# A two-layer hybrid backbone step: the next head pair's r, k, v projections moved into a pair's tail, four-quadrant small matmuls, and low weight halves made by accumulating transfers

## The reference, cut to what matters

```python
h = rmsnorm(x, g_pre) * (1 + sc1) + sh1          # sc, sh, g: rows of silu(c) @ ada_w + b
z = h @ w_in                                     # projections of three mixers, and gates
out_a = rwkv7(dwconv3(z[r, k, v, w, a, g]))      # bidirectional delta-rule scan, 8 heads of 64
out_b = neighbourhood_attention(z[q, k, v])      # or dense, for the context; softmax
out_c = chunkwise_retention(z[q, k, v, g])       # bidirectional
merged = sum(sigmoid(z[gate_i]) * out_i @ w_o_i)
x = x + g1 * rmsnorm(merged @ w_out, g_post)
h2 = rmsnorm(x, g_ffn) * (1 + sc2) + sh2
x = x + g2 * rmsnorm((gelu(gate) * val) @ ffn_down, g_post2)  # gate, val = split(dwconv3(h2 @ ffn_up))
```

## Time and profile before

| | |
|---|---|
| median of 3 runs | 2025.21 us (2020.05 to 2028.73) |
| the profiled execution | 2030.75 us, span 2028.6 us |
| PE busy | 1905.9 us (94%) |
| DVE, ACT, POOL busy | 1001.8, 939.8, 944.0 us |
| moved by DMA | 231.52 MB, mean 114 GB/s |

### The profile page before, as it was taken

The page is one execution under the profiler, slowest core; times in us unless marked ns, Lnnn a source line. Parts: engine busy times, 40 slices in busy tenths (PEclk is TensorE's granted clock), DMA queues, the critical chain, the costliest instruction groups (busy, mean ns, idle before and its releaser), DMA issues.

```text
span 2028.6 us, 41739 instructions
## 1 busy us (share of the span) xinstructions
PE 1905.9 (94%) x17940; PEld 1718.9 (85%) x17940; DVE 1001.8 (49%) x1516; ACT 939.8 (46%) x1766; POOL 944.0 (47%) x767
## 2 busy tenths in 40 slices
PE   6899999999999989999988999999999998999997
PEld 2887878797899879999947878787879997899996
DVE  2574747475611255552057657475745133555502
ACT  4554645454533454443345555364554334544432
POOL 1434426170666626666416153342516664466663
PEclk9999999999999989999989999999999999999998
DMA  7314232232443314434453141413224432244442
GB/s 291 101 50 143 64 117 94 89 115 86 135 124 122 120 63 124 124 122 127 123 204 124 50 140 55 136 65 125 87 88 156 125 125 83 94 125 125 125 125 73
DMA packets 65414, 231.52 MB, mean 114 GB/s; under 512 B 7376, under 2 KB 11856, under 8 KB 64592
## 3 DMA queue, kind: packets, MB, share of 16 engines
q1 hardware_dynamic: 59040, 215.21, 33.3%
q10 hardware_dynamic: 6192, 13.66, 1.9%
HBM read 223.58 MB, written 5.26 MB: 113 GB/s over the span
## 4 chain that ended last, share of the span: by engine, by line
PE 79%; DVE 9%; ACT 4%; issue 3%; POOL 2%; DMA 2%; ACTq 1%; SPq 0%; DVEq 0%; POOLq 0%
PE psz L471 57%; PE psw L471 20%; DVE work L1360 3%; ACT work L954 3%; DMA ring<-in_w 2%; POOL ringlo L1735 1%; DVE work L1369 1%; PE psz L479 1%; PE psw L479 1%; ACT whi L954 1%; DVE rstd L1369 1%; DVE part L1360 1%; DVE work L1363 1%; POOL work L1771 1%; DVE work L1366 0%
## 5 line engine op out<-in xcount | busy, mean ns | idle before, releaser
L1735 POOL TENSOR_TENSOR ringlo<-ring,whi 128x512 fp32r<-128x512 f32 x608 | 811.1, 1357 | 756.7 <-ACT whi L954 756.7
L471 PE MATMUL psz<-hhi,whi 128*128 128x386 f32 x1696 | 587.1, 346 | 23.2 <-POOL ringlo L1735 14.5
L471 PE MATMUL psz<-hlo,whi 128*128 128x386 f32 x1696 | 577.6, 341 | 0.0
L471 PE MATMUL psz<-hhi,ringlo 128*128 128x386 f32 x1696 | 576.4, 340 | 0.0
L954 ACT ACTIVATE whi<-ring 128x1024 fp32r<-128x1024 f32 x304 | 320.2, 1053 | 133.4 <-PE psz L471 125.1
L471 PE MATMUL psw<-work 64*64 64x64 f32 (+4 forms) x9024 | 348.8, 232 | 17.6 <-issue 9.1
L471 PEld LDWEIGHTS psw<-work 64*64 64x64 f32 (+2 forms) x9024 | 294.5, 137 | 73.1 <-issue 55.6
L471 PEld LDWEIGHTS psz<-hhi,whi 128*128 128x128 f32 x1696 | 321.0, 189 | 36.1 <-issue 18.9
L471 PE MATMUL psz<-part,whi 128*128 128x386 f32 x1344 | 346.6, 339 | 3.2 <-DVE work L1360 1.5
L471 PEld LDWEIGHTS psz<-hlo,whi 128*128 128x128 f32 x1696 | 322.9, 190 | 2.1
L471 PEld LDWEIGHTS psz<-hhi,ringlo 128*128 128x128 f32 x1696 | 321.0, 189 | 0.0
(11 more groups left out here) (107 smaller groups left out, 1725.2 us busy)
## 6 DMA issues: line engine op xcount, KB each, us to landing
ring<-in_w SPq DMA_DIRECT2D x400, 512.0 KB, 3.5
pk<-in_pk ACTq DMA_DIRECT2D x8, 832.0 KB, 4.4
const<-in_const SPq DMA_DIRECT2D x1, 1795.0 KB, 10.0
work<-in_x SPq DMA_DIRECT2D x1, 1544.0 KB, 6.8
work<-in_x ACTq DMA_DIRECT2D x1, 1544.0 KB, 6.5
out_x<-work ACTq DMA_DIRECT2D x1, 1544.0 KB, 5.5
work<-out_x ACTq DMA_DIRECT2D x1, 1544.0 KB, 9.8
out_x<-work SPq DMA_DIRECT2D x4, 386.0 KB, 2.3
```

The costliest lines, as they stand in the source:

```text
L471: ins = nc.tensor.matmul(out, a, b, start=start, stop=stop, skip_group_check=True)
L1735: L.do(G.tensor_tensor(out, a, b, op), S[sig] if sig else None)
```

## The change

1. **Quadrants.** gl, xt, g0, wm and u loop `for x: for hb: for c:`, and the second head of the pair (hb = 1) has its partition halves crossed, so that four products in a row lie in four quadrants. For this DVE makes the crossed transposes (`across`, two instructions of 64 partitions for hb = 1), once after level 0 and once in each of levels 1 to 4; `gl` and `xt` wait for both heads at once. ACT copies `art` in three parts instead of one.
2. **r, k, v of pair p+1 in the tail of pair p** (`next_steps`, 24 steps of three matmuls, cut as 2, 3, 3, 3, 2, 4, 3, 4 between the tail's steps; three pairs of four), with their ACT copies and splits (`next_tap`) and DVE taps there. A later pair's front has 7 dense columns. The ada steps move from the tail into levels 4 and 5 (3 + 3 and 4 + 4, then 2). The order of the weight stream stays.
3. **Order of the front.** For p > 0: key sums, nq, lora, nk, nv, rq, rk, rv, rg; `g_up` later; softmax steps 0, 1, 2 one dense column later each. On DVE the norms of the pair before (`scale_rwkv`, `scale_ret`, `finish_*`) and the softmax steps 0 and 1 lie between the two directions of the scan and after it.
4. **Low halves.** `split(j)` writes `whi` and then minus the same into the ring slot with a second ACT instruction; `low(j)` is then one accumulating DMA on POOL's queue that adds the 512 KB block from HBM to the slot. One semaphore per slot (`w_low`).
5. The first ada stage uses four groups of columns of 256 instead of two of 512 at a time, with the sum of squares in one place. The pack of a pair is loaded in two parts.

```diff
-                        for i in range(p == 0, 5):
-                            dense(zb + i, bb + i)
...
+                            key_sums()
+                            dense(zb + ZI["nq"], bb + 3)
...
+                            lora_up()
+                            dense(zb + ZI["nk"], bb + 4)
+                        dense(zb + ZI["nv"], bb + 5)
+                        dense(zb + ZI["rq"], bb + 6)
...
+                            pe.wait_ge(*at_of("x_ready", p, 0 if lv == 1 else 2 * (lv - 2) + 2))
+                            for x in range(6):
+                                for hb in range(2):
                                     for c in range(2):
-                                        mm(psw[hc(c), g_bank(lv, hb), CH * x:CH * x + CH], au[hc(c), hb, x, 0, 0:CH],
+                                        mm(psw[hc(c ^ hb), g_bank(lv, hb), CH * x:CH * x + CH], au[hc(c), hb, x, 0, 0:CH],
                                            xv[hc(c), hb, x, :], sig="gl_done" if (x, c) == (5, 1) else None)
...
                                 retain(lv - 4)
-                                if lv == LEVELS - 1:
-                                    ada_steps(2)
...
+                                ada_steps(3 if lv == 4 else 4)
...
                         retain(2)
-                        ada_steps(4)
...
+                        ada_steps(2)
+                        next_steps(2)
...
-                        ada_steps(2)
+                        next_steps(3)
...
-                        run(high(j), ring[:, b % RING * 1024:(b % RING + 1) * 1024], sig="w_hi")
+                        raw = ring[:, b % RING * 1024:(b % RING + 1) * 1024]
+                        run(high(j), raw)
+                        run(wlo[b % RING], raw, ACT.Copy, "w_hi", scale=-1.0)
...
+                            else:
+                                split(sb_ + 10)
...
+                        def next_tap(i):
+
+                            if p + 1 < PAIRS:
+                                centre_tap((rc, kc_, vc)[i], zb + ZI["r"] + i, "conv", 4 * i + p + 1)
+                                split(sb_ + 13 + i)
...
+                    def across():
+
+                        for c in range(2):
+                            flip(tvv[hc(1 - c), 1:2], xv[hc(c), 1:2], "tv_ready" if c else None)
...
+                            if p:
+                                (scale_rwkv, scale_ret)[d](p - 1)
+                            if d:
+                                attend(0)
+                                if p:
+                                    finish_ret(p - 1)
...
-                        for i in range(2):
-                            part_ = slice(512 * i, 512 * i + 512)
-                            tt(wlo[a][:, part_], ring[:, a * 1024 + 512 * i:a * 1024 + 512 * i + 512],
-                               high(j)[:, part_].bitcast(F32), ALU.subtract, sig="w_lo")
+                        pool.dma_start(wlo[a], wstream[layer, SPLIT[j]],
+                                       accum_op=ALU.add).then_inc(w_low[a].h, 16)
```

More of the change, by code:

```diff
@@ L1080, in _, with query_in @@
[L1080 to L1081 removed]
+                        if p == 0:
+                            for i, dst in enumerate((rc, kc_, vc)):
+                                centre_tap(dst, ZP + i, "conv", 4 * i)
+                                split(sb_ + i + 3)
+                        def query_in():
+                            seen(zb + ZI["nq"])
+                            run(nq, z(zb + ZI["nq"]), free=zb + ZI["nq"], scale=0.125)
+                            split(sb_ + 6)
@@ new lines, in key_in, with key_root @@
+                        def key_in():
+                            seen(zb + ZI["nk"])
+                            if p:
+                                act.wait_ge(*after("out_k", 32 * p))
+                            run(nk, z(zb + ZI["nk"]), free=zb + ZI["nk"])
+                            L.settle()
+                            act.dma_start(nak[layer, p], nk[:, 0:P]).then_inc(S["out_k"].h, 16)
+                            split(sb_ + 7)
+                        def key_root():
+                            act.wait_ge(*at_of("kkn_done", p, 0))
+                            run(Px, w(0), ACT.Sqrt, "kkn_root")
```

418 lines of the change are left out of this document (236 added, 182 removed).

## The result

The changed kernel takes 2330.5 us (median of 4 runs, 2321.8 to 2334.7), the kernel before in the same rounds 2023.1 (2020.1 to 2028.7): 15.1% slower, ratio 1.1506 with a 95% interval of 1.1475 to 1.1536. I had predicted 1987 with 1932 to 2095, so sign and size were both wrong.

The account below looks back on a forecast made before the run. It took PE to run the dense stages at its own pace, so only the pairs could win. Terms -47 - 8 - 24 + 7 + 29 + 12 - 4 - 3 = -38 us against 2025.2 gave 1987 us, range 1932 to 2095.

Parts of the forecast that it names:

- L: Low halves: time from the second ACT instruction's end until the block may be used; taken as 5.0 us, bounds 3.5 and 7.0.
- rival C: Dense stages: the accumulating transfer sets the pace once L is over 5.8 us; 2101 us at L = 7, chance 0.24.
- part 1: Quadrants in the pairs: eight groups save 0.73 us of issue each, 5.8 us per pair, -47 us in eight.
- part 5: Last stretch before layer 1's ada rows: shrinks by about 4 us with half the time per block and sums ahead.
- part 2b: Next pair's r, k, v steps fill the tail's idle PE time: 4.0 us in each of six pairs, -24 us.
- rival B: Later pairs' front: DVE bounds it, 5 us per pair instead of 2, and filling falls short; 2020 us, chance 0.14.
- L = 5.0 just fits: cost 0: Dense stages: 5.9 or 5.1 us are left for L, so the transfer costs nothing, with nearly no slack.
- my 14 places: Waits for r's weights, fronts and FFN starts: +2 us each in 14 places at L = 7, +28 us.
- Rival D: Quadrant groups: PE fetches weights for four quadrants at no better rate; 2034 us, chance counted within rival B's 0.14.
- The wait for r's weights: Tail: PE waits 4.8 us for the next r block's low half, six times, +29 us.
- Part 3: Later pairs' front: 1 us wait for rk's low half and 1 us at `am`, +12 us in six pairs.
- Part 2a: Ada steps moved from the tail into levels 4 and 5: net -1.0 us per pair, -8 us.

Follow-up runs that it names:

- e1_sub: The changed kernel with the low halves again made by two subtractions on POOL, all else as changed; 2037.5 us, ratio 1.0052 to the kernel before.
- e2_acc: The kernel before with only the second ACT instruction and the accumulating transfer for low halves put in; 2330.4 us, ratio 1.1512.

## Why the accumulating transfer is late

Five kernels take the transfer apart. *e3_plain* keeps both ACT instructions and the transfer, but the transfer doesn't add (`accum_op` is left out); *e4_act* is e1_sub with ACT writing the high half twice, so that only ACT's cost is left. *g1_half* makes every second low half by the transfer and the others by POOL; *g2_warm* and *g3_warm1* put dummy matmuls ahead of PE's waits.

```diff
-                        pool.dma_start(wlo[a], wstream[layer, SPLIT[j]],
-                                       accum_op=ALU.add).then_inc(w_low[a].h, 16)
+                        pool.dma_start(wlo[a], wstream[layer, SPLIT[j]]).then_inc(w_low[a].h, 16)
```

```diff
+                        run(high(j), raw)
+                        L.settle()
                         run(high(j), raw, sig="w_hi")
```

```diff
+                        if j % 2 == 0:
+                            pool.dma_start(wlo[a], wstream[layer, SPLIT[j]],
+                                           accum_op=ALU.add).then_inc(w_low[a].h, 16)
+                            return
+                        for i in range(2):
...
```

```diff
+                        if j >= SM + 9 and j not in (SO + 2,):
+                            keep_warm(8)
                         out = opened(zi)
                         pe.wait_ge(*low_in(j))
```

The diffs are those of e3_plain, e4_act (against e1_sub), g1_half and g2_warm, in this order; g3_warm1 has `keep_warm(1)`. e3_plain leaves the subtraction out: its low half is the rounded weight itself.

*e3_plain*, expected:

> The changed kernel in which POOL's transfer is a plain load of the same 512 KB over the slot instead of an accumulating one; the low half is then the rounded weight, so the output is not the reference's. It parts the add from the queue. Theory T1 (it is the add: the doubled reading): landing 4 to 5 us, DMA share in FFN near 0.6, PE near its pace: 1990 to 2050 us. Rival T2 (it is POOL's issue and completion, or the queue on the same 16 engines): landing stays near 7 us and the time above 2200 us.

*e4_act*, expected:

> e1 with ACT writing each high half twice (two instructions of 1.05 us and the wait between them, as long as the changed kernel's pair), low halves by POOL's subtraction. It prices ACT's share of part 4 alone. Theory T: splits have slack in the dense stages, ACT costs up to 20 us over e1, from the pairs. Rival T3 (ACT's longer split is itself a main cause): 80 us or more over e1.

*g1_half*, expected:

> Kernel: the changed kernel in which only every second block gets its low half by the accumulating transfer (two ACT instructions, one DMA), the others by POOL's subtraction as before. Theory D (throughput: a low half takes two transfers' worth and more of the DMA engines, whose share is 0.85 in the FFN and grows to queueing, so that the landing takes 7 to 10 us instead of 5.5): with half of them the share falls to about 0.6, a transfer lands in 5 to 6 us, and each has a cheap block beside it; nearly all of the loss goes: 2045 to 2090 us. Rival M (latency of each accumulate alone, whatever else the queues carry): every second block still pays its 1.35 us: half of the loss, 2037 + 146 = 2183 us.

Measured: e3_plain 2114.3 us, ratio 1.0428 (1.0409 to 1.0447); e4_act 2066.8, ratio 1.0192 (1.0150 to 1.0234); g1_half 2151.3, ratio 1.0619 (1.0585 to 1.0652). All three lie above what I expected, e3_plain between its two theories. The page of e3_plain and, in a stretch of its FFN, the chain:

```profile
q1 hardware_dynamic: 59040, 215.21, 29.8%
q0 software_dynamic: 43776, 159.40, 26.1%
...
ringlo<-in_w POOLq DMA_DIRECT2D x304, 512.0 KB, 4.4
```

```profile
810.35 49.77 PE psz L488 x280
```

With the same bytes read from memory and no addition, a transfer lands in 4.4 us, and this stretch of the FFN runs at PE's pace, 49.77 / 280 = 0.178 us per matmul. The addition is what costs most. In time of all 16 DMA engines a transfer takes 0.261 x 2117.3 / 304 = 1.82 us without it (span 2117.3) and 0.402 x 2332.9 / 304 = 3.09 us with it, and a plain load 0.256 x 2332.9 / 410 = 1.46 us (215.21 MB are 410 blocks of 524 KB). The same plain loads took 0.333 x 2028.6 / 410 = 1.65 us in the kernel before, so such a figure is good to some 10%. Per block of the FFN that is 4.5 us with the addition, more than PE's 4.27, and 3.3 without. The landing goes from 4.4 to 6.8 us, the time by 216 of the 293 us. ACT's second instruction is 29 of it by e4_act; a POOL-issued plain transfer in place of POOL's subtraction the remaining 48.

The chain of g1_half in the FFN, its stretch, its queue 0 and its landing:

```profile
862.00 17.22 PE psz L490 x96
...
879.32 17.22 PE psz L490 x96
```

```profile
828.00:1100.00 272.00, 259.56 (x1494) 243.23 (x1493) 83.46 (x134) 136.87 (x201) 92.67 (x81) 0.98 0.73 192
...
q0 software_dynamic: 21888, 79.70, 22.7%
...
ringlo<-in_w POOLq DMA_DIRECT2D x152, 512.0 KB, 5.5
```

With half of the adds (1.54 + 1.60 us of DMA time per block on average, by the same sums) the steady FFN is back at PE's pace, 96 matmuls in 17.22 us, and a transfer lands in 5.5 us by the median of the whole kernel. The cheap blocks between would not do that alone: at L = 8.6 a column with an addition would follow the column three before it by 2.6 + 8.6 + 4.27 us, and that one its neighbour by 4.27, which makes 4.9 us per block. So L fell with the load, and in the dense stages, where it had grown from some 6 to 8.6, the loss is mainly one of load. The DMA engines are not the limit by themselves there (share 0.86); their load enters through L. Between the marks of the dense stages g1_half is 29 us above e1_sub, where the changed kernel is 174 above. The expectation of 2045 to 2090 was still missed by 61 us, because the pairs pay for latency, load or not: in g1_half the third pair takes 121.6 us (362.87 to 484.50), as in the changed kernel (120.2), against 110.3 in e1_sub. In the chain of g1_half's pair, with the queues quiet, stands

```profile
411.89 5.81 DMA ringlo<-in_w
```

which with 0.29 and 0.14 us around it is L = 6.2, already over the 5.8 from which rival C's loss begins. PE's waits for a transfer in the third pair of the changed kernel (us in all, times, longest), and the busy times of that pair in the changed kernel and in e1_sub:

```profile
PE psz L488 <- DMA ringlo<-in_w: 8.8, 2, 6.3
```

```profile
372.31:492.52 120.21, 103.86 (x1533) 86.97 (x1532) 65.49 (x122) 66.79 (x139) 22.77 (x30) 0.94 0.53 133
...
340.64:450.90 110.26, 100.19 (x1534) 83.54 (x1533) 71.76 (x123) 57.45 (x129) 42.04 (x40) 0.98 0.31 97
```

The two waits are 6.3 us at the next pair's first r step and 2.6 at rk's column, where e1_sub has 2.3 us and none. That is 6.5 of the 9.9 us. The other 3.7 are longer PE busy time for the same matmuls, at a granted clock of 0.94 instead of 0.98.

*g2_warm* and *g3_warm1*, expected:

> Kernel: the changed kernel (2330.5 us) with eight dummy matmuls of 256 columns on constants put ahead of each dense column's wait for the low half in gates, output and FFN (some 1.0 us at full clock, which fit into the 1.3 us or more that PE waits there). They add work but keep PE active. Theory K (a part of the loss is TensorE at 1.2 GHz behind the waits: the mean granted clock is 0.928 against 0.982): PE is then granted the full clock throughout, the groups of 48 in 10.3 to 11.5 us return to 8.5, and the time falls by 30 to 100 us: 2230 to 2300 us, clock above 0.96. Rival T (the transfers alone set the pace and half-clock matmuls lie inside the wait): clock up, time unchanged within 10 us or longer by up to 30: 2320 to 2360 us.

> Kernel: the changed kernel (2330.5 us) as in g2_warm, but with one dummy (two instructions, 0.45 us) instead of eight (16 instructions, 3.62 us by g2_warm's trace, far more than the wait that they were to fill) ahead of each dense column's wait. Theory K (a part of the loss is TensorE at 1.2 GHz behind the waits): clock above 0.94, time 10 to 40 us less, 2290 to 2320 us. Rival T (the transfers alone set the pace): unchanged within 10 us, 2320 to 2340.

Measured: g2_warm 2626.8 us, ratio 1.2988 (1.2962 to 1.3014), clock 0.952; g3_warm1 2300.4, ratio 1.1355 (1.1315 to 1.1395), clock 0.936. The first was sized wrongly. I had taken eight dummies for 1.0 us, and its trace shows 3.62:

```profile
904.47 3.62 PE L488 MATMUL psw<-const 128*128 128x256 f32 x16
```

Far more than the wait, so PE paid for them; its stretch from 900 to 1100 us has a granted clock of 1.00 and no wait for a transfer. With one dummy (0.45 us) the kernel is 30 us faster than the changed one, although PE does more. The gain lies where the dummies are: from the first branch product to the first product of FFN down it takes 444.4 us in layer 0 and 447.7 in layer 1, at clock 0.96 in layer 0, where the changed kernel takes 464.9 and 461.8, at 0.93. (I had expected a clock above 0.94 over the whole kernel; it is 0.936.) So some 30 of the 293 us go away with nothing changed but what PE does ahead of its waits, and the granted clock is what moved with it. How much the lower level costs in all is open; PE's busy time for the same 18068 matmuls is 1947.2 us in the changed kernel and 1862.2 in e1_sub, so 85 us is an estimate of the most that it can be.

## Why the other parts brought nothing

PE's waits say it. One pair (the third of layer 0, from the first matmuls on the pack, softmax step 1, to the same of the next pair): the kernel before, then e1_sub (engine waited for: us in all, times, longest us).

```profile
PE psw L471 <- ACT work L954: 2.3, 3, 1.1
PE psw L471 <- issue: 1.5, 1, 1.5
PE psw L471 <- DVE work L1360: 0.6, 1, 0.6
PE psz L471 <- POOL ringlo L1735: 0.4, 1, 0.4
PE psw L471 <- DVE work L1376: 0.3, 1, 0.3
```

```profile
PE psw L483 <- DVE work L1459: 3.0, 4, 1.7
PE psz L483 <- POOL ringlo L1852: 2.3, 1, 2.3
PE psw L491 <- ACT mix L1002: 2.1, 1, 2.1
PE psz L483 <- ACT work L1002: 1.5, 1, 1.5
PE psw L483 <- DVE work L1447: 0.5, 1, 0.5
PE psw L483 <- DVE work L1463: 0.5, 1, 0.5
PE psw L483 <- ACT work L1002: 0.3, 1, 0.3
```

The tail's 3.8 us of waits for ACT and issue are gone, as I had said. But 5.1 us in all have become 10.2. L1459 is DVE's masked copy in the levels, `ringlo` the low half of the next r, `mix` a softmax step's copy at level 1, and the wait on psz for `work` lies ahead of `g_up`, now at the front's end. The period is 110.3 us instead of 110.8, with less busy PE time (100.2 us instead of 105.5) and more waits. The next runs try them.

*f1_late* takes away the wait for r (first steps later, the split behind the copies of wm and u); *f2_two* uncrosses the second head of e1_sub; *h1_part1* is the kernel before with part 1 alone; *h3_ada* is f1_late with the old first ada stage.

```diff
-                        next_steps(2)
...
-                        next_steps(3)
+                        next_steps(5)
...
-                            else:
-                                split(sb_ + 10)
...
+                        split(sb_ + 10)
                         late_rows(p, zb + ZI["ada"])
```

```diff
-                                    mm(psw[hc(c ^ hb), g_bank(lv, hb), CH * x:CH * x + CH], au[hc(c), hb, x, 0, 0:CH],
+                                    mm(psw[hc(c), g_bank(lv, hb), CH * x:CH * x + CH], au[hc(c), hb, x, 0, 0:CH],
```

```diff
-                    for b in range(2 * KT):
-                        if b == (10 if layer else 6):
-                            sum_squares(0)
...
+                            for i in range(2):
+                                j = 2 * jp + i
+                                mm(psw[32 * j:32 * j + 2, 1, :], cs[:, k, :], ring2[b % RING][:, i, :], k == 0,
+                                   k == KT - 1, "row_done" if k == KT - 1 else None)
```

The diffs are those of f1_late, f2_two (one of its lines; xt, g0, wm, u, art and `across` likewise) and h3_ada. h1_part1 has the lines of the change's part 1 and nothing else of it.

> Kernel: the changed kernel with POOL's subtraction back (as e1_sub, 2037.5 us), and in the tail the first two of the next pair's r steps are done three positions later (0, 3, 3, 5 at the start instead of 2, 3, 3, 3), while the split of r's weights stands behind the copies of wm and u in ACT's program instead of inside level 5. Theory W (in e1_sub PE waits 2.26 us at the first r step for the low half, and the half clock behind it costs about 1.5 us more, in six pairs): the wait and the half-speed matmuls vanish, 3 to 4 us in each of six pairs, 18 to 24 us: 2014 to 2020 us, about as fast as the kernel before. Rival V (the tail is bound by its own small steps and by DVE, and the wait merely covers them): under 6 us, 2031 to 2038 us.

> Kernel: e1_sub (2037.5 us) with the second head of a pair no longer crossed: the same order of instructions and the same number of DVE and ACT instructions, but all groups gl, xt, g0, wm, u in two quadrants. Theory P (since DVE's masked copies and transposes and ACT's copies now set the period of a level, a group of 48 in 0.93 instead of 1.6 us is worth little; only g0, wm, u and a part of gl count): 3 x 0.68 us x 8 = 16 us and at most as much again for gl, 2045 to 2065 us. Rival Q (quadrants give what I took, 5.8 us per pair, and the loss lies elsewhere): +47 us, 2084 us. Rival N (nothing is gained at all): 2037 us within 4.

> Kernel: the kernel before with part 1 alone: gl, xt, g0, wm, u in four quadrants, with the crossed transposes on DVE (three transposes of 0.57 to 0.62 us per level, 1.79 us together, instead of one of 0.98). Theory P (the level's period is then DVE's, as e1_sub's rows show; f2_two against e1_sub gives 0.8% for the quadrants themselves, about 17 us, and DVE's extra 0.8 us in four levels of eight pairs takes up to 26 us of it where DVE is on the path): 2010 to 2030 us, within 0.5% of before. Rival Q (the loss of e1_sub comes wholly from the moved steps and the first ada stage, and part 1 brings what I took): 1976 us.

> Kernel: f1_late (2035.2 us) with part 5's ada stage undone: two groups of 512 columns at a time, rows copied as soon as each is done, the squares summed between the blocks. In the traces the first lora of layer 0 stands at 110.5 us before and at 115.8 in e1_sub, and in layer 1 the stretch from the end of the FFN to it is 3 us longer too. Theory (part 5 costs some 8 us where I predicted a gain of 4, since the squares stand late in one place and all four rows come at the end): 2027 us within 4, that is 0.4% less. Rival (the later lora is due to the order of the front): 2035 us within 3.

Measured, with the ratio to the kernel before: f1_late 2035.2 us, 1.0045 (1.0023 to 1.0067); f2_two 2050.3, 1.0134 (1.0118 to 1.0150); h1_part1 2034.6, 1.0046 (1.0024 to 1.0068); h3_ada 2027.5, 1.0010 (0.9994 to 1.0025).

*f1_late*: the wait for r goes and nothing is won, as its rival V said. Where e1_sub has 2.26 us for POOL's low half, f1_late stands for 2.32 us some products further on, in the middle of `nn`. PE's row, and ACT's copies of wm and u:

```profile
388.58 0.94 PE L483 MATMUL psw<-work 64*64 64x64 f32 x49 [2.32 <-issue]
...
382.21 1.64 ACT L1001 ACTIVATE work<-psw 128x384 f32<-128x384 f32 x4 [4.59 <-PE psw L483]
```

The copies end at 383.85, so PE doesn't wait for u. It stands for nothing that the profile names: such idle time (`issue`) adds up to 18.0 us over the whole of f1_late against 4.1 in e1_sub for products into psw, while that behind POOL's low halves falls from 24.9 to 14.5. A load of 16 KB of instructions (queue 8, 386.0 to 386.5) lies at its start. In five of the six such gaps of 1.6 us or more in this run a load of this kind begins, or in the microsecond before; one comes every 14 us. That they cause the gaps is not shown.

*f2_two* came out within its range: in e1_sub the quadrants themselves are worth 0.8%, 17 us, where I took 47. *h1_part1*, 5 us above its expected range, shows why part 1 is worth less than that. PE's waits in its third pair:

```profile
PE psw L471 <- DVE work L1376: 5.1, 5, 1.7
PE psw L471 <- ACT work L955: 2.3, 3, 1.1
PE psw L479 <- ACT mix L955: 2.1, 1, 2.1
```

DVE's masked copies, for which PE did not wait before, now end 5.1 us of idle time per pair, and a softmax step's copy 2.1: 7.2 us of new waits against 5.8 us saved in issue. A group of 48 does fall from 1.61 to 0.93 us. But DVE then has, in each of four levels, three transposes of 0.57 us in place of one of 0.98, and the softmax and decay-table work that PE's longer groups used to hide. I had looked at one gap, from gl to xt with 2.1 us of cover, and not at DVE's queue over a whole level.

*h3_ada*: 7 us less than f1_late, ratios with intervals that just touch. The traces don't put this into the ada stage: the first softmax step 1 of layer 0 stands at 114.2 us in f1_late and 114.0 in h3_ada (110.5 before, where it comes one dense column of 4.27 us earlier in the front), and the difference is spread over pairs. So part 5 shows no worth in the stage itself, neither the -4 I took nor the +8 I then expected, though one execution doesn't tell 2 us (the same kernel has that mark at 114.1 in k1_cross and at 115.9 in l2_again). The expected time came true by luck, and what the 7 us are stays open.

## Relieving DVE, and the filling of the tail

If DVE's queue sets the time of a level, the crossing belongs elsewhere. *h2_actx* (on the kernel before) and *k1_cross* (on h3_ada) let ACT cross the second head back when it copies gl's result, so that xt keeps two quadrants and DVE its one transpose:

```diff
-                            run(gg.rearrange("p h x c -> p h (x c)"), psw[:, b:b + 2, 0:384], sig="gl_ready")
+                            run(gg[:, 0], six(psw[:, b, 0:384]))
+                            run(gg[hc(0), 1], six(psw[hc(1), b + 1, 0:384]))
+                            run(gg[hc(1), 1], six(psw[hc(0), b + 1, 0:384]), sig="gl_ready")
```

In h2_actx the last masked copy leaves the uncrossed old values of the second head beside the crossed new ones, so what it computes after that is another thing, with the same instructions; k1_cross and l1_quad transpose crossed once, at level 4, which sets that right. *k2_table* is k1_cross with the decay tables' four DVE instructions at the begin of the front; *k4_small* is the kernel before with k2_table's two edits; *l1_quad* is k4_small without the moved tables; *l2_again* is k1_cross beside it. *k3_end* is h3_ada with all steps, copies and taps of the next r, k, v at the tail's end. The diffs below are k2_table's and k3_end's.

```diff
-                            if lv == 2:
-                                for hb in range(2):
-                                    i = 8 + 2 * p + hb
-                                    ts(dtab[:, hb, :], cv("dist", 384), lg[:, i + 8:i + 9], -1.0, op1=ALU.mult)
...
+                        for hb in range(2):
+                            i = 8 + 2 * p + hb
+                            ts(dtab[:, hb, :], cv("dist", 384), lg[:, i + 8:i + 9], -1.0, op1=ALU.mult)
...
                         dve.wait_ge(*after("kkn_root", p + 1))
```

```diff
-                            if n < 2:
-                                next_steps(3)
...
-                        next_steps(4)
+                        next_steps(24)
```

> Kernel: the kernel before with four quadrants in gl, g0, the last xt, wm and u, and no crossed transposes: ACT crosses the second head's halves back when it copies gl's result (three instructions instead of one, some 0.5 us more beside PE's softmax step), xt of levels 1 to 4 stays in two quadrants as before. DVE has exactly the work of before. Theory P (DVE's added 0.8 us per level eats the quadrants' gain): eight groups of 24 products save 0.68 us each per pair, 43 us at most, of which DVE's and ACT's waits take a third or so: 1985 to 2005 us, faster than both kernels. Rival D2 (DVE's old work, 5 us per level, is already the period): 2010 to 2023 us, no more than h1_part1.

> Kernel: h3_ada (2027.5 us) in which DVE makes the crossed transposes only at level 4; in levels 1 to 3 ACT crosses the second head back when it copies gl's result, xt keeps two quadrants there, and DVE makes one transpose of 0.98 us instead of three of 1.79. Theory P (in a level PE waits for DVE's queue, up to 1.7 us at gl, and each DVE instruction added there lengthens the pair): four times 0.8 to 1.1 us less DVE work per pair gives 2 to 3.5 us in each of eight pairs, 1999 to 2012 us. Rival (DVE's waits move to ACT's three copies, as two rows of the run with ACT's crossings on the kernel before show PE waiting 0.3 to 0.5 us for ACT): 2018 to 2027 us.

> Kernel: k1_cross with the four DVE instructions of the decay tables (0.42 + 0.62 us for each of two heads, 2.1 us) moved from level 2 to the begin of the front. In h3_ada PE waits 1.68 us for DVE's masked copy right behind them. Theory P (the level's period is DVE's queue): 1.0 to 1.7 us less in each of eight pairs, 8 to 14 us less than k1_cross. Rival (the time comes back in the front, where DVE is busy for 74% before the change): within 3 us of k1_cross.

> Kernel: h3_ada (2027.5 us) with part 2b's filling undone: the 24 steps of the next pair's r, k, v, ACT's copies with their splits, and DVE's taps all stand at the tail's end instead of between its small steps. Theory F (the filling works as predicted, 4.0 us of idle PE in each of six tails): 2027 + 24 = 2051 us, and more clock lost. Rival G (the tail's idle is small and the steps only lengthen the waits of the chain of small products and copies): 2020 to 2032 us.

> Kernel: the kernel before with two of the ideas alone: four quadrants with ACT's crossings in levels 1 to 3 (DVE's at level 4 only), and the decay tables moved to the begin of the front; no moved projections, no new order of the front, the old ada stage, POOL's subtraction. Theory P: the quadrants' 5.8 us per pair are now partly free, as DVE is relieved by 1.3 us in level 2; 1.5 to 3 us in each of eight pairs, 2002 to 2014 us. Rival (nothing, as in h1_part1 which gave 2034.6): 2023 to 2030 us.

> Kernel: the kernel before with the quadrants alone, crossed by ACT in levels 1 to 3 and by DVE at level 4, the tables in their old place (k4_small without its moved tables). Theory: k4_small's loss (2043.4 us) is the tables in front of the front's DVE work, as k2_table's against k1_cross was 14.5 us; without them the quadrants give 1.5 to 2 us in each of eight pairs: 2008 to 2016 us. Rival (ACT's three copies, or the crossing itself, cost what the quadrants give on the old front and tail): 2020 to 2028 us.

> Kernel: k1_cross once more, beside l1_quad and with more rounds, to tell the two apart. Theory F (the moved projections fill the tail, worth 22 us by k3_end against h3_ada, and cost some of it in the levels and the front): 5 to 12 us less than l1_quad, 2010 to 2014 us, 0.5 to 0.7% faster than before. Rival (the moves are worth nothing net): within 3 us of l1_quad.

| kernel | us | ratio to before (95%) |
|---|---|---|
| h2_actx | 2019.2 | 0.9972 (0.9954 to 0.9990) |
| k1_cross | 2012.8 | 0.9939 (0.9912 to 0.9967) |
| k2_table | 2027.4 | 1.0013 (0.9999 to 1.0027) |
| k3_end | 2049.7 | 1.0125 (1.0100 to 1.0150) |
| k4_small | 2043.4 | 1.0082 (1.0057 to 1.0107) |
| l1_quad | 2018.3 | 0.9968 (0.9955 to 0.9981) |
| l2_again | 2015.9 | 0.9949 (0.9934 to 0.9965) |

Against what I expected: h2_actx fell to its rival D2, k1_cross and l1_quad came out a few us above their ranges, k2_table and k4_small missed both of their ranges, k3_end was as expected. l2_again is 2.4 us below l1_quad, within the 3 us of its rival.

*k1_cross* is faster than both kernels, by 0.5 to 0.6% of the kernel before in two measurements, 10 us or so. That is little, but both intervals lie below 1. PE's waits in its third pair:

```profile
PE psw L483 <- issue: 1.5, 1, 1.5
PE psz L483 <- ACT work L1008: 1.5, 1, 1.5
PE psw L483 <- ACT work L1008: 0.8, 2, 0.5
PE psw L491 <- ACT mix L1008: 0.7, 1, 0.7
PE psw L483 <- DVE work L1469: 0.7, 2, 0.5
```

The masked copy (L1469 here) ends 0.7 us of idle time instead of e1_sub's 3.0, the softmax copy 0.7 instead of 2.1. The pair takes 107.6 us (328.82 to 436.44) against 110.8 before; the granted clock of that stretch is 1.00, against 0.97 in h3_ada's.

*k2_table* refutes what I had expected of the tables: 15 us more than k1_cross. Its third period is 109.7 us, 2.1 more, the DVE time of the four instructions (2 x (0.42 + 0.62)); all six together are 16 us longer. In the level they were hidden once the crossing was off DVE; in the front nothing hides them. On the old front the same move costs 25 us (k4_small against l1_quad). So in both fronts added DVE work lengthens the pair, which is the mechanism of rival B.

*k3_end* confirms one term: without the filling h3_ada is 22 us slower, and I had taken 24 for it. The tail's waits are back in its list of the third pair, 2.6 us for ACT, 1.9 of issue and 1.1 for DVE.

*l1_quad* against *l2_again*: the two differ by 0.2%, with intervals that overlap. The moved projections with the new order of the front are worth 2 to 6 us on top of the quadrants by the medians (l2_again, k1_cross), which is not clear of noise. The marks of one execution each show where the filling's gain goes: the six periods are 13 us shorter in l2_again (323.7 and 326.4 against 331.7 and 331.4 us for three), and the layers' starts up to the first mark 7.1 us longer in each layer, of which the last pairs give back 3.2 in all. Of each 7.1, 4.3 are that the mark comes one dense column later; the last pair should give these back and doesn't.

## Why the prediction was wrong

*What bounds the kernel.* Right: the dense stages at PE's pace, the pairs alone to gain. I read there that POOL's time is hidden, and costed part 4's removal at nothing, which is right too.

*The miss.* It is 343 us. Some 80 lie in the other parts, -69 taken and +10 measured. Some 260 lie in part 4: 31 us were taken for it over POOL's subtraction (-38 against -69), and 293 measured.

*Part 4, the step that failed.* It is "I take L = 3.5 + 1.5 = 5.0", from which followed "L = 5.0 just fits: cost 0". The mechanism, a loop over three blocks, was right, and this term was mis-sized, by which the sign went. Measured: 6.2 with quiet queues, 8.6 in the FFN, beyond the upper bound of 7.0. With L = 8.6 my own formula gives (2.6 + 8.6 + 4.27) / 3 = 5.16 us per block, and the trace has 5.15. In 220 blocks that is (5.16 - 4.27) x 220 = 196 us, where the marks show 198. That they meet so closely is partly luck, as FFN down loses only 0.5 us per block and the stages ahead of it more. Two choices made L small. I added the destination's reading as 1.5 us of bytes at the flooded rate, while e3_plain against the changed kernel shows 2.4 us. And I took the landing of a plain load at a DMA share of 0.40, while part 4 itself brings the share to 0.86. I had set 4.5 us of DMA time per block against 4.27 as a bound, by three times the bytes at the flooded rate, and left it to rival C because packets overlap better than in the flood. They don't when they add: 4.5 us is what the queues' shares give.

Outside the dense stages I had 31 us, with 17 more at L = 6.2 by my 14 places at 1 us per us, so 48; the marks show 102. The places in a pair were right: the first r step and rk's column. My price for them over e1_sub's is 3.4 + 1 us at L = 5 and 6.8 at L = 6.2, and the third pair has 6.5. Two terms were put at nothing. One is PE's lower clock behind waits, 3.7 us in that pair. The other is the start of a layer, where I wrote that the wait "costs nothing": PE waits there 20 us for added blocks in layer 0 against 5 for POOL's in e1_sub, and the first mark comes 14 us later in layer 0 and 12 in layer 1. The last pairs, +21, were not looked into.

The Trainium skill (DMA: Bandwidth & Descriptors, Anatomy of one DMA; Collectives: The Full Stack, The bandwidth ceiling) gave an estimate of 4.4 us in my reading, which by my 14 places would lower the sum by 8 us, not by some 5. The halved rate agrees roughly: an addition takes 1.7 times the DMA time of the same POOL transfer without it, and 2.1 times that of SP's plain load. The latency does not: 5.8 us on a quiet queue and 6.8 by the median, so for this transfer the measurement decides. As to the warning in the Trainium skill (SBUF — State Buffer, SBUF: two separate sides), no run here shows transfers held up by DVE, nor was one made for it.

*Rivals.* C was it, at 0.24; its price of 2101 was the price of the bound L = 7. The prediction named the sign itself, L beyond 5.8. C's "for it" said that two bounds lie just at the pace. With a price whose slope is 87 us per us and a value that no row shows, slack of 0.1 us at the likeliest value is no slack, and C deserved more than a half.

*Part 1.* -47 taken; the quadrants give 17 (f2_two), and with DVE's crossing +9 (h1_part1). The step that failed is "DVE's `across` adds about half a transpose per level beside PE's softmax step": it adds 0.7 us (three of 0.57 against one of 0.98), and the cover was that of one gap, not of DVE's queue. Rival D was wrong: the quadrants issue at 0.93 us per 48.

*Part 2b.* -24 for the filling: right, 22. The wait for r's weights, 4.8 by my count, is 2.3 in e1_sub and 6.3 in the changed kernel. Removing e1_sub's gives nothing (f1_late), since idle time that the profile doesn't explain comes in its place. Of the 3.7 us of idle rows that I wanted to fill, 1.47 were of this kind, and k1_cross still has 1.5.

*Part 3.* +2 us per front taken; e1_sub's new wait there, ahead of `g_up`, is 1.5 us (the 2.1 us at level 1 are part 1's, since h1_part1 has them too). Rival B's mechanism, DVE in the front, is what k2_table shows. That the first pair of a layer, which has nothing moved ahead of it, pays for the new order without the gain would fit l2_again's marks, but was not tried.

*Parts 2a and 5.* Small in the sum. Part 2a was not tried alone; part 5 is not to be told from nothing in its own stage. DVE's instructions did get faster without POOL, `mix<-mix` from 1282 to 561 ns, which agrees with the contention that the Trainium skill states (SBUF — State Buffer, Who interferes with whom) for a DVE instruction with two SBUF inputs beside a GpSimd instruction that reads SBUF. It moved nothing that PE waited for.

## What to carry to other kernels

A transfer in a loop is costed at the load that it makes itself, and an operation that the trace doesn't hold at the far bound when the slope behind it is steep: measure it alone before building on it. A wait of PE costs more than its length when the clock falls behind it, so compare PE's busy time for the same matmuls. When an engine's groups get shorter, list PE's waits over one whole period and add up the queue of each helper engine; the gap that covered the helper's work is made of the time that is being saved. Filling waits with moved work does what it promises in its place, and is worth only what the places it is moved from don't ask back.

## What the runs showed of the hardware

An accumulating transfer of 512 KB into SBUF took 5.8 us on a quiet queue and 6.8 to 7.0 by the median of a whole kernel (changed kernel, e2_acc), and 0.87 us of POOL to issue. The same transfer without the addition took 4.4 (e3_plain). The addition took 2.1 times the DMA time per MB of SP's plain loads; without it (e3_plain, 26.1 / 159.40 against 29.8 / 215.21) POOL's transfers still took 1.2 times. Plain loads beside it slowed from 3.6 us (e1_sub) to 5.4. One dummy of 0.45 us ahead of PE's waits made a kernel 30 us faster, and the same 18068 matmuls kept PE busy for 1947.2 us with the waits and 1862.2 without. A DVE transpose of 64 partitions by 384 takes 0.57 us, as long as one of 128 partitions.
